# Layer A of a two-layer decoder: sixteen attention maps moved by DMA in four sets, multiplied with v in two visits

## The reference

```python
qkv = (x @ a_w_qkv[layer]).reshape(B, S, 3, A_HEADS, A_HEAD_DIM)
q, k = rotary(q), rotary(k)                      # first 16 of 64 columns
s = einsum("hqd,hld->hql", q, k) / 8, masked to l <= q
o = softmax(s) @ v                               # 16 heads, 256 x 256 maps
x = layer_norm(ALPHA * x + o @ a_w_o[layer])
x = layer_norm(ALPHA * x + conv_ffn(x))
```

## Time and profile before

| | us |
|---|---|
| median of 3 runs | 590.10 (589.78 to 590.34) |
| profiled execution | 591.97 |
| its span, first to last instruction | 590.0 |
| TensorE busy | 579.2 (98%) |
| VectorE busy | 449.7 (76%) |
| ScalarE busy | 334.5 (57%) |
| GpSimd busy | 50.4 (9%) |
| mean granted TensorE clock | 0.997 |

### The profile page before, as it was taken

One profiled execution on the slowest core, in us unless ns is written; L12 is line 12 of the kernel. 1 busy time (PEld: TensorE's weight loads), 2 busy tenths in 40 slices (PEclk: granted clock), 3 DMA queues, 4 the chain that ended last, 5 costly groups with the idle time before them and its releaser, 6 DMA issues.

```text
span 590.0 us, 7746 instructions
## 1 busy us (share of the span) xinstructions
PE 579.2 (98%) x2714; PEld 473.1 (80%) x2714; DVE 449.7 (76%) x819; ACT 334.5 (57%) x560; POOL 50.4 (9%) x84
## 2 busy tenths in 40 slices
PE   8999999999999999999999999999999999999995
PEld 6887777888878888888888888888888888888884
DVE  3889996876688868667879796778767888766656
ACT  4767585245566656554545678945555565555530
POOL 5300000400000000000130003132000000000003
PEclk9999999999999999999999999999999999999998
DMA  8897967456668897866457865442965889777511
GB/s 302 295 311 235 278 174 248 142 181 198 192 210 264 274 344 229 269 223 207 158 195 228 300 173 177 141 143 73 305 192 179 251 254 329 247 242 246 179 36 72
DMA packets 96242, 128.26 MB, mean 217 GB/s; under 512 B 13468, under 2 KB 74188, under 8 KB 96204
## 3 DMA queue, kind: packets, MB, share of 16 engines
q1 hardware_dynamic: 94764, 123.58, 65.9%
q0 software_dynamic: 1152, 4.19, 2.0%
q10 hardware_dynamic: 288, 0.00, 0.0%
HBM read 108.23 MB, written 1.05 MB: 185 GB/s over the span
## 4 chain that ended last, share of the span: by engine, by line
PE 88%; DVE 4%; DMA 3%; ACT 2%; SPq 1%; issue 1%; DVEq 0%
PE wide L1321 18%; PE wide L1323 17%; PE wide L1322 17%; PE score L1322 5%; PE score L1323 5%; PE score L1321 5%; PE turn L1321 3%; PE turn L1322 3%; PE outb L1322 3%; PE turn L1323 3%; PE outb L1323 3%; PE outb L1321 3%; DVE w_lo L1000 2%; DMA kT<-turned 2%; ACT w_hi L803 1%; DMA xs<-in_x 1%
## 5 line engine op out<-in xcount | busy, mean ns | idle before, releaser
L1000 DVE TENSOR_TENSOR w_lo<-raw,w_hi 128x2048 fp32r<-128x2048 f32 (+1 forms) x120 | 210.7, 1776 | 59.4 <-ACT w_hi L803 59.1
L803 ACT ACTIVATE w_hi<-raw 128x2048 fp32r<-128x2048 f32 (+1 forms) x126 | 184.2, 1488 | 92.7 <-PE wide L1323 44.8
L1321 PE MATMUL wide<-w_hi,oT_hi 128*128 128x512 f32 x240 | 94.7, 395 | 0.0
L1323 PE MATMUL wide<-w_hi,oT_lo 128*128 128x512 f32 x240 | 93.5, 390 | 0.0
L1322 PE MATMUL wide<-w_lo,oT_hi 128*128 128x512 f32 x240 | 93.4, 389 | 0.0
L1321 PE MATMUL wide<-w_hi,xT 128*128 128x512 f32 x224 | 89.8, 401 | 0.5 <-DVE xT L1025 0.3
L1323 PE MATMUL wide<-w_hi,xT 128*128 128x512 f32 x224 | 87.4, 390 | 0.0
L1322 PE MATMUL wide<-w_lo,xT 128*128 128x512 f32 x224 | 87.3, 390 | 0.0
L1321 PE MATMUL score<-w_hi,xT 128*128 128x512 f32 x160 | 62.2, 389 | 0.0
L1322 PE MATMUL score<-w_lo,xT 128*128 128x512 f32 x160 | 62.2, 389 | 0.0
L1323 PE MATMUL score<-w_hi,xT 128*128 128x512 f32 x160 | 62.2, 389 | 0.0
(11 more groups left out here) (170 smaller groups left out, 836.9 us busy)
## 6 DMA issues: line engine op xcount, KB each, us to landing
raw<-in_ffn_w_in SPq DMA_DIRECT2D x88, 512.0 KB, 5.4
raw<-in_ffn_w_out SPq DMA_DIRECT2D x22, 1024.0 KB, 7.4
kT<-turned SPq DMA_DIRECT2D x104, 128.0 KB, 2.8
raw<-in_a_w_qkv SPq DMA_DIRECT2D x9, 1024.0 KB, 7.6
raw<-in_w_kv_shared SPq DMA_DIRECT2D x8, 1024.0 KB, 5.9
raw<-in_a_w_o SPq DMA_DIRECT2D x4, 1024.0 KB, 6.6
raw<-in_b_w_q SPq DMA_DIRECT2D x4, 1024.0 KB, 5.0
raw<-in_b_w_o SPq DMA_DIRECT2D x4, 1024.0 KB, 5.0
```

Source lines behind the costliest of these rows:

```text
L803: ins = nc.scalar.activation(w_hi[c % RING][:, part], raw[c % RAW_RING][:, part], ACT.Copy)
L1000: ins = nc.vector.tensor_tensor(w_lo[c % RING][:, part], raw[c % RAW_RING][:, part], w_hi[c % RING][:, part].bitcast(F32), ALU.subtract)
L1321: nc.tensor.matmul(dst, a_hi, b_hi, start=start, stop=False, skip_group_check=True)
L1323: return nc.tensor.matmul(dst, a_lo, b_hi, start=False, stop=stop, skip_group_check=True)
```

## The change

All sixteen maps of layer A go through VectorE's transposes and the DMAs, in four sets of four; TensorE's transposes of maps 14 and 15 and ScalarE's copies of them are gone from layer A, key tile 7 takes the block order, and all of layer A uses one causal mask. There are four pv groups, one for each set, and their results go by turns into two PSUM banks (`out_bank`, `turn_bank`). In the planner scores 3 now need transfer 1, pv 0 and pv 1 both need transfer 1, and pv 2 and pv 3 both need transfer 3. In the queue itself pv m waits for the transfer of set m alone (each set has its own semaphore), and scores 3 for no transfer. wo kt needs out_lo kt // 2.

```diff
@@ mixer_schedule
+            if A and m == 12:
+                after[("scores", 3)].append(("prob_move", 1))
...
-            if m < MOVED:
-                add(("prob_turn", m), ("norm", m))
...
-                if m % BATCH == BATCH - 1 or m == MOVED - 1:
-                    add(("prob_move", n), ("prob_turn", m), ("prob_move", n - 1), ("pv", n - 2))
-            else:
-                add(("probT", m), ("norm", m))
-                add(("probT_out", m), ("probT", m), ("pv", 1))
+            add(("prob_turn", m), ("norm", m))
...
+            if m % BATCH == BATCH - 1:
+                add(("prob_move", n), ("prob_turn", m), ("prob_move", n - 1))
+                after[("prob_move", n)] += [("pv", n - 2)] if n >= 2 else []
...
-        if A and m % 2 and m in [heads[-1] for heads in PV_GROUPS]:
-            n = PAIR_GROUP[m // 2]
-            add(("pv", n), *[("prob_move", h // BATCH) if h < MOVED else ("probT_out", h) for h in PV_GROUPS[n]], ("drain", column(2, g), 1), ("out_lo", n - 1) if n + 1 < len(PV_GROUPS) else ("probT_out", m))
-            add(("out_hi", n), ("pv", n))
-            add(("out_lo", n), ("out_hi", n))
+        if A and n % VISITS == VISITS - 1 and m % BATCH == BATCH - 1:
+            for k in range(n - VISITS + 1, n + 1):
+                add(("pv", k), ("prob_move", n), ("drain", column(2, k // 2), 1), ("out_lo", k - 2))
+                add(("out_hi", k), ("pv", k))
+                add(("out_lo", k), ("out_hi", k))
...
-                after[("wo", kt, st, half)].append(("out_lo", PAIR_GROUP[kt] if A else kt))
-    after[("split_hi", first_chunk + 17, 0)].append(("out_hi", PAIR_GROUP[7] if A else 7))
+                after[("wo", kt, st, half)].append(("out_lo", kt // 2 if A else kt))
+    after[("split_hi", first_chunk + 17, 0)].append(("out_hi", SETS - 1 if A else 7))
     if A:
-        after[("split_lo", first_chunk + 16, 0)].append(("out_lo", PAIR_GROUP[6]))
+        after[("split_lo", first_chunk + 16, 0)].append(("out_lo", SETS - 1))
...
-        elif step == ("prob_move", MOVED // BATCH):
-            takes = 3.0
+        elif step == ("prob_move", SETS - 1):
+            takes = 1.9
@@ yoco_trunk
+    def group_bank(n):
+
+        return (out_bank, turn_bank)[n % 2]
...
-                maps = min(BATCH, MOVED - BATCH * n)
-                sp.wait_ge(prob_turned, BATCH * n + maps)
+                sp.wait_ge(prob_turned, BATCH * (n + 1))
...
-                                 ).then_inc(prob_moved[n % 2], 16)
+                                 ).then_inc(prob_moved[n], 16)
...
-                        newest = PV_GROUPS[m][-1] if layer == 0 else m
-                        if layer == 0 and newest < MOVED:
-                            n = newest // BATCH
-                            pe.wait_ge(prob_moved[n % 2], 64 * (n // 2 + 1))
+                        if layer == 0:
+                            pe.wait_ge(prob_moved[m], 64)
...
-                            elif m < len(PV_GROUPS) - 1:
-                                pe.wait_ge(olo_done, m)
+                            elif m >= 2:
+                                pe.wait_ge(olo_done, m - 1)
...
-                                pe.wait_ge(olo_done, PAIR_GROUP[kt] + 1)
+                                pe.wait_ge(olo_done, kt // 2 + 1)
```

More of the change, by code:

```diff
@@ L38 @@
 X_ORDER = (0, 2, 1, 3)
-BATCH, MOVED = 4, 14
+BATCH = 4
 HIDDEN = 4
@@ L89 @@
 }
-PV_GROUPS = ((0, 1, 2, 3), (4, 5, 6, 7), (8, 9, 10, 11), (12, 13), (14, 15))
-PAIR_GROUP = [n for n, heads in enumerate(PV_GROUPS) for _ in heads[::2]]
+SETS = 16 // BATCH
+VISITS = 2
 LAG = {"move": 3.0, "prob_move": 3.0}
@@ L290, in mixer_schedule @@
             takes = 1.1
-        if A and step[0] in ("pv", "out_hi", "out_lo") and len(PV_GROUPS[step[1]]) == 4:
+        if A and step[0] in ("pv", "out_hi", "out_lo"):
             takes = {"pv": 1.65, "out_hi": 0.5, "out_lo": 0.62}[step[0]]
-        elif A and step[0] == "pv":
-            takes = 1.0
-        elif step == ("prob_move", MOVED // BATCH):
-            takes = 3.0
+        elif step == ("prob_move", SETS - 1):
+            takes = 1.9
         (products_left if step[0] in ("proj", "wo") else waiting[step[0]]).pop(0)
@@ L459, in yoco_trunk @@
                       qk_rows[:, 0:BATCH * 3 * P]]
-        prob_stage = [stage.rearrange("p (b s k q) -> p b s k q", b=4, s=BATCH, k=3) for stage in prob_stage]
-        prob_stage.append(turned[:, :, :, :].rearrange("p n b q -> p (n b q)")[:, 0:(MOVED % BATCH) * 3 * P]
-                          .rearrange("p (b s k q) -> p b s k q", b=4, s=MOVED % BATCH, k=3))
+        prob_stage = [prob_stage[n].rearrange("p (b s k q) -> p b s k q", b=4, s=BATCH, k=3) for n in (0, 1, 2, 1)]
         conv_rows = sb("conv_rows", [4 * FT, LAYERS, P])
@@ L520, in yoco_trunk @@
         turn_filled, turn_drained, turned_done = sem("turn_filled"), sem("turn_drained"), sem("turned_done")
-        prob_turned, prob_moved = sem("prob_turned"), [sem(f"prob_moved{n}") for n in range(2)]
+        prob_turned, prob_moved = sem("prob_turned"), [sem(f"prob_moved{n}") for n in range(SETS)]
         moved = {(mat, g): sem(f"moved_{'qk'[mat]}{g}") for mat in range(2) for g in range(2)}
@@ L588, in prob_move @@
                 for a in range(4):
-                    part = slice(a * maps * 3 * 32, (a + 1) * maps * 3 * 32)
+                    part = slice(a * BATCH * 3 * 32, (a + 1) * BATCH * 3 * 32)
                     sp.dma_start(probsT_A[n % 2][:, part],
                                  prob_stage[n][32 * a:32 * a + 32].rearrange("p b s k q -> p b (s k q)")
-                                 ).then_inc(prob_moved[n % 2], 16)
+                                 ).then_inc(prob_moved[n], 16)
             def in_move(layer, i):
@@ L871, in _ @@
                             act.wait_ge(prob_turned, m - 3)
-                        elif layer == 1 and MAPS - 4 + m < MOVED:
+                        elif layer == 1 and m < 4:
                             act.wait_ge(prob_turned, MAPS - 4 + m + 1)
-                        elif layer == 1 and m < 4:
-                            act.wait_ge(turn_filled, fill_of[(0, "probT", MAPS - 4 + m)] + 1)
                         elif layer == 1:
@@ L1130, in _ @@
                             if mat and layer == 0:
-                                tiles = 4 if COLUMNS[m][1] == 0 else MOVED // 2 - 4
-                                for t in range(tiles):
+                                for t in range(4):
                                     into = parts[:, :, 64 * t + 32 * st:64 * t + 32 * st + 32].rearrange("p b (n i) -> p b i n", n=4)
                                     last = nc.vector.transpose(into, tokens[:, :, 2 * t:2 * t + 2, :])
-                                if tiles < 4:
-                                    into = parts.rearrange("p b (t s q) -> p b t s q", t=4, s=ST)
-                                    last = nc.vector.transpose(into[:, :, tiles:4, st, :], tokens[:, :, 2 * tiles:8, :])
                             elif mat:
@@ L1152, in _ @@
                             last = nc.vector.tensor_tensor_reduce(
-                                out=masked[:, m % 2, lo:hi], in0=score_banks[m % 4][:, lo:hi], in1=causal[0 if j < MOVED else 1][:, lo:hi],
+                                out=masked[:, m % 2, lo:hi], in0=score_banks[m % 4][:, lo:hi], in1=causal[layer][:, lo:hi],
                                 scale=-SCALE, scalar=3e38, op0=ALU.add, op1=ALU.min,
@@ L1208, in _ @@
                     elif kind == "out_lo":
-                        dve.wait_ge(ohi_done, len(PV_GROUPS) * layer + m + 1)
+                        dve.wait_ge(ohi_done, SETS * layer + m + 1)
                         if layer == 0:
@@ L1419, in _ @@
                         n = fill_of[(layer, "probT", m)]
-                        slot = 2 * (m % 2) if layer else m % 4
+                        slot = 2 * (m % 2)
                         pe.wait_ge(norm_done, MAPS * layer + m + 1)
@@ L1439, in _ @@
                                 pe.wait_ge(cols_drained, 1)
-                            elif m < len(PV_GROUPS) - 1:
-                                pe.wait_ge(olo_done, m)
[L1442 to L1449, removed]
+                            elif m >= 2:
+                                pe.wait_ge(olo_done, m - 1)
+                            turned_probs = probsT_A[m % 2].rearrange("p (a s k q) -> p s k a q", a=4, s=BATCH, k=3)
+                            bank = group_bank(m)
+                            for n in range(BATCH // 2):
+                                head = BATCH * m + 2 * n
                                 part = [bank[0:64, n * SEQ:(n + 1) * SEQ], bank[64:P, n * SEQ:(n + 1) * SEQ]]
@@ L1463, in _ @@
                             if m == 0:
[L1464 removed]
+                                pe.wait_ge(olo_done, SETS)
                             else:
```

28 lines of the change are left out of this document (12 added, 16 removed).

## The result

The changed kernel takes 591.65 us (median of 7, 591.42 to 592.1), the one before 590.08 (589.75 to 590.46): ratio 1.0026, 95% interval 1.0017 to 1.0035, or +1.6 us. The forecast was +0.9, with the range up to 592.6.

What follows compares the result with a forecast made beforehand. TensorE's instruction stream was taken as the bound. 1.8 us saved, about 2.6 of stalls (three of 0.85) and 0.1 of rounding gave +0.9, so 590.1 + 0.9 = 591.0 us; range 588.8 to 592.6.

Steps and rivals of the forecast that it cites:

- transfer 3: Last transfer of maps, awaited by pv 3: starts at 94.2, takes 5.8 us, is there at 100.0.
- A: The forecast case: VectorE's queue sets transfer 3, +0.9 us, own range 590.5 to 591.4; chance 0.50.
- D: Slower: VectorE's chain is longer than worked out; with 6.05 for the transfer +2.3, 592.4; chance 0.23.
- The order: Order of every engine's queue in layer A's attention, worked through with the planner's own costs.
- VectorE's chain: VectorE's queue from 72.73 us, by pitches, never short of input: turns 14 and 15 end at 94.2.
- The gaps at wo 0 and wo 2: TensorE waits for out_lo 0 and out_lo 1, 0.85 us each; time pv 3 would have waited anyway.
- The saving: TensorE: three visits fewer at 0.40 us each and 0.61 for turning maps 14 and 15, 1.8 us saved.
- The page's figure for a transfer: About 2.0 us fixed plus bytes over 436 GB/s: 2.45 us for 192 KB, transfer 3 there at 99.05, no wait.
- B: Transfer 3 is in time while both out_lo waits stay: -0.1 us, 590.0; chance 0.13.
- C: No wait of TensorE at all, so the full gain: 588.3; chance 0.12.
- E: Stalls cost TensorE clock, nothing until a gap is several us; then 2 to 4 us more; chance 0.02.
- F: Visits are not merged because a product slips between: 0.4 us each, within A's range; no chance of its own.

Runs made afterwards that it cites:

- wo by pairs: Changed kernel with kt 0 and 1 of both halves of wo's first token tile before kt 2 and 3 on TensorE: 591.72 us, ratio 1.0027.
- the repetition: The changed kernel measured again with no edit, against the kernel before: 592.0 us, ratio 1.0036.
- all of it together: Changed kernel, three half splits behind turn 15, wo by pairs, norm 13 before out_lo 1, ScalarE's half splits of 15 behind exp 15: 589.13 us, ratio 0.9982.

## Why the prediction was right, and where it was short

The mechanism, the sign and the whole range held; the size was short by 0.7 us, +0.9 against +1.57, because one term, the time of transfer 3, was taken too small. The result lies above A's own range, 590.5 to 591.4, and inside the whole one only since that reached up to the end of D, whose longer chain did not happen: that it was covered is in part luck. "Slower", which its median is by the 0.2% of the prediction, had a chance of 0.38, and "the same" 0.50.

**The order.** The queues worked out from the planner's table are those of the changed kernel, step for step.

**VectorE's chain.** Turn 15 was forecast to end at 94.2, or 93.7 after the 0.49 by which this trace is early; it ended at 93.70. The pitches of the earlier trace rows carried it, and VectorE never waited on the way.

**The gaps at wo 0 and wo 2.** Forecast 0.85 each, counted from where a product could have started: measured 85.35 - 84.55 = 0.80 and 87.74 - 86.84 = 0.90. That the second costs nothing by itself is shown by the run with wo by pairs.

**The saving.** Forecast 1.8. The gaps are 0.80, 0.90 and 100.43 - 98.85 = 1.58 at pv 3, with 0.11 and 0.05 of slower restart behind the last two; the stretch grew by 1.86, so 3.44 - 1.86 = 1.6 were saved. The fastest kernel gives the same: its gaps are 0.2 and 0.62, with 0.05 of restart, and 30.37 - (29.65 - 0.87) = 1.6. If the turns were worth their 0.61, which no run took alone, a visit less is worth 0.33, not 0.40: the slower products behind a visit should not have been added, or not in full. It did not matter, as the last wait absorbs the difference.

**The term that was mis-sized: transfer 3.** Forecast 5.8 us, ends 5.4 and 6.1; measured 6.6, in the repetition 6.45, and 6.4 to 6.7 in the other runs with one queue in which pv 3 waited, but for the one with load 18 held back. I built the term from transfer 1, whose four issues took 3.01, which leaves 2.8 from the end of the last issue to the arrival. Here the issues took 3.37, as one of them took 1.43 where the longest of transfer 1 took 1.02, and 3.26 passed behind them. The long issue is the smaller part: with wo by pairs and with all of it together the four issues took 3.07 and 3.12, about as in transfer 1, and pv 3 came after 6.37 and 6.41 all the same, 3.3 behind the last issue. I noted that load 18 comes behind transfer 3, but not that it starts while the last part is on its way; with it held back 2.83 passed behind the issues and 6.1 in all, in one trace. So the piece behind the last issue was taken some 0.4 too short, and by that one trace load 18 accounts for 0.3 to 0.4 of it, which the time did not confirm; the rest stays open.

These 0.8 us, and 0.1 between turn 15's end and the first issue (93.70 to 93.80), which I had at nothing, are the difference at pv 3: measured from scores 2, it was forecast at 29.86 and came at 30.78, and wo 4 followed 1.45 behind it, as forecast. The 0.34 that the kernel before loses at 168 us, and the others do not, bring the 1.86 of the stretch to 1.5, beside the measured 1.57. Why it loses them was not followed up.

**The page's figure for a transfer.** The fit of the Trainium skill, DMA: Bandwidth & Descriptors, section Anatomy of one DMA, is made for transfers that GpSimd issues, while SyncE issues these. By it pv 3 would not have waited, and the time would have been about 590.0, an estimate. The measurement decides against it again: the quickest part of transfer 3 took 3.1 us.

**The rivals.** B and C are what the edits to the queue reach, not the change itself. With the half split of 15 behind turn 15 the kernel is near to B: both waits for out_lo and 0.30 at pv 3, 590.41 where B had 590.0. C's full gain, 588.3, was not reached by any kernel; the fastest, 589.13, still has 0.8 us of gaps and saves 1.6 instead of 1.8. D, a longer chain on VectorE, did not happen: turn 15 ended when A said. Of D only the longer transfer came true. E, the clock, did not happen in the two traces of the changed kernel, whose gaps of 1.42 and 1.24 us left it at 1.00; but its premise, no effect until a gap is several us, does not hold in the run with two queues (below). F did not happen.

## What to carry to other kernels

Follow the last semaphore before the joint, and find what stands ahead of it in its producer's queue: three half splits, which TensorE did not need before wo 4, 8 us behind turn 15, cost this change its gain, and moving them behind turned +1.6 us into -0.6. Do not add up gaps on one queue; one that comes before a wait on an independent chain can be free: here the last wait grew by what was taken away. A greedy planner fills what it sees as a gap with work that is not urgent; where its products are slower than the chip's (0.8 and 0.75 against 0.68 us here), that gap may not exist. This last point is a reading of its table, which no run tested.

## What the runs showed of the hardware

A second issuing queue did not shorten a transfer in four parts of 192 KB: with two parts each on SyncE's and ScalarE's queue, the second issue took 1.6 to 1.7 us on both, and the slowest part landed 6.5 us after its issue, against 3.1 to 4.0 with all four on one queue in the changed kernel. That is one trace of a long execution; the median, 592.51, says only that nothing was gained.

With all four parts on one queue the four issues took 3.07 to 3.65 us in the eight traces in which pv 3 waited, and one of the four was long every time, 0.99 to 1.76 against 0.54 to 0.79 of the other three. From the end of the last issue to pv 3 it was 2.9 to 3.3 us, and 2.8 with load 18 held back. The two that had the shortest issues:

```profile
93.71 3.07 SPq L591 DMA_DIRECT2D spare<-turned  x4
```

```profile
90.96 3.12 SPq L595 DMA_DIRECT2D spare<-turned  x4
```

The granted clock can fall after 2 us without a matmul, which I had priced only for gaps of several us. In the trace with two queues, behind a gap of 2.04 us (98.42 to 100.45), it was still 1.00 in the first half us of matmuls and then fell: 0.58 in the stretch from 101, and 0.50 (1.2 GHz) until past 104, over 3 us in all, with products 0.42 apart instead of 0.23:

```profile
100.00:101.00 1.00, 0.55 (x6) 0.40 (x8) 0.00 (x0) 0.00 (x0) 0.00 (x0) 1.00 1.06 374
101.00:102.00 1.00, 1.00 (x12) 0.64 (x10) 0.00 (x0) 0.00 (x0) 0.00 (x0) 0.58 0.75 266
102.00:103.00 1.00, 1.00 (x7) 0.67 (x4) 0.00 (x0) 0.31 (x1) 0.00 (x0) 0.50 0.16 54
```

In the run with wo by pairs a gap of 2.16 us at the same place left it at 1.00, so a gap of that length makes the fall possible, not certain. What decides between the two was not settled. At the end of the kernel before, 1.00 had lasted until 587, over 4 us behind the last product (582.47), longer than in the run with two queues. The Trainium skill, TensorE: Matmul & The Clock Gate, section HAM oscillation, says that idle gaps throttle the engine; the trace with two queues agrees in kind, the one with wo by pairs does not show it.
